# The beginning of a streaming encoder step: meta rows as 128 short rows, gain row spread by a product, forget-gate columns in four blocks, two weight units interleaved

## The reference

```
xn = x * rsqrt(mean(x*x) + 1e-6) * g_pre_mix            # every row, meta rows too
y  = xn @ w_in        # columns: fox q | k | v | 8 forget logits | swa q | k | v | gates
logf = log_sigmoid(f + b_forget);  c = cumsum(logf)      # bias of the fox attention
... fox attention (8 heads), window attention, output mix, MLP
```

## Time and profile before

| what | us |
|---|---|
| median of 3 runs (1680.64 to 1680.95) | 1680.81 |
| the profiled execution, its own time | 1680.76 |
| its span from first to last instruction | 1679.0 |
| TensorE (PE) busy | 1651.5 |
| DVE busy | 1083.5 |
| ACT busy | 775.8 |
| POOL busy | 310.2 |

### The profile page before, as it was taken

The page is one execution under the profiler, slowest core; times in us unless marked ns, Lnnn a source line. Parts: engine busy times, 40 slices in busy tenths (PEclk is TensorE's granted clock), DMA queues, the critical chain, the costliest instruction groups (busy, mean ns, idle before and its releaser), DMA issues.

```text
span 1679.0 us, 27411 instructions
## 1 busy us (share of the span) xinstructions
PE 1651.5 (98%) x9540; PEld 1489.3 (89%) x9540; DVE 1083.5 (65%) x2322; ACT 775.8 (46%) x1630; POOL 310.2 (18%) x438
## 2 busy tenths in 40 slices
PE   8999999999999999999999999999999999999998
PEld 8999999999999988989988899888888888888886
DVE  7556666553999744454445597888877667774744
ACT  6477777765777533352233333222222334443521
POOL 1311111115333211124532230000000000000242
PEclk9999999999999999999999999999999999999999
DMA  5221212231222554563443422444432763444641
GB/s 187 77 61 41 79 47 59 67 110 36 74 57 67 163 179 160 160 210 123 147 140 111 134 85 94 131 144 144 144 131 105 258 220 111 132 149 125 192 163 75
DMA packets 164314, 205.34 MB, mean 122 GB/s; under 512 B 16152, under 2 KB 113240, under 8 KB 164208
## 3 DMA queue, kind: packets, MB, share of 16 engines
q1 hardware_dynamic: 164208, 203.97, 38.0%
HBM read 144.85 MB, written 57.28 MB: 120 GB/s over the span
## 4 chain that ended last, share of the span: by engine, by line
PE 80%; DVE 9%; ACT 4%; issue 4%; POOL 2%; DMA 0%; DVEq 0%; ACTq 0%; SPq 0%; POOLq 0%
PE gb L503 8%; PE gb L3173 6%; PE gb L2290 5%; PE sc L3173 5%; PE gb L2825 4%; PE gb L2661 4%; PE sc L2825 4%; PE tp L3173 4%; PE tp L2825 4%; PE tp L798 3%; PE sc L2449 3%; PE tp L2449 3%; PE gb L930 3%; PE gb L931 2%; PE gb L932 2%
## 5 line engine op out<-in xcount | busy, mean ns | idle before, releaser
L930 PE MATMUL gb<-Xh,wh 128*128 128x384 f32 (+1 forms) x504 | 175.9, 349 | 0.0
L489 POOL TENSOR_TENSOR wl<-raw,wh 128x256 fp32r<-128x256 f32 x168 | 125.0, 775 | 264.2 <-ACT wh L474 175.4
L931 PE MATMUL gb<-Xh,wl 128*128 128x384 f32 (+1 forms) x504 | 170.7, 339 | 0.0
L932 PE MATMUL gb<-Xl,wh 128*128 128x384 f32 (+1 forms) x504 | 170.7, 339 | 0.0
L3297 POOL TENSOR_TENSOR wl<-raw,wh 128x1024 fp32r<-128x1024 f32 x2 | 5.3, 2626 | 559.0 <-ACT wh L3288 559.0
L503 PE MATMUL gb<-Xh,wh 128*128 128x384 f32 (+1 forms) x288 | 103.9, 361 | 0.0
L503 PE MATMUL gb<-Xh,wl 128*128 128x384 f32 (+1 forms) x288 | 97.4, 338 | 0.0
L503 PE MATMUL gb<-Xl,wh 128*128 128x384 f32 (+1 forms) x288 | 97.3, 338 | 0.0
L930 PEld LDWEIGHTS gb<-Xh,wh 128*128 128x128 f32 x504 | 95.0, 189 | 0.1
L931 PEld LDWEIGHTS gb<-Xh,wl 128*128 128x128 f32 x504 | 95.0, 188 | 0.0
L932 PEld LDWEIGHTS gb<-Xl,wh 128*128 128x128 f32 x504 | 94.8, 188 | 0.0
(11 more groups left out here) (548 smaller groups left out, 4777.4 us busy)
## 6 DMA issues: line engine op xcount, KB each, us to landing
zr<-u_scr SPq DMA_DIRECT2D x91, 256.0 KB, 3.0
raw<-in_w_in SPq DMA_DIRECT2D x70, 256.0 KB, 3.2
u_scr<-ustore SPq DMA_DIRECT2D x26, 576.0 KB, 3.6
u_scr<-ustore SPq DMA_DIRECT2D x13, 768.0 KB, 3.2
sig_scr<-sig SPq DMA_DIRECT2D x16, 576.0 KB, 3.1
raw<-in_w_up SPq DMA_DIRECT2D x36, 256.0 KB, 4.4
kc<-in_cache_fox_k SPq DMA_DIRECT2D x8, 1024.0 KB, 5.6
vc<-in_cache_fox_v SPq DMA_DIRECT2D x8, 1024.0 KB, 7.6
```

Of the source, the lines that this page charges most:

```text
L489: nc.gpsimd.tensor_tensor(wl[U.slot][:, q], raw[U.slot][:, q], wh[U.slot][:, q].bitcast(F32), ALU.subtract).then_inc(w_lo if x == 3 else w ...
L930: nc.tensor.matmul(gb[c][:, 0:x1 - x0], wh[U.slot][:, ws], Xh3[:, k, x0:x1], start=(k == 0), stop=False)
L931: nc.tensor.matmul(gb[c][:, 0:x1 - x0], wl[U.slot][:, ws], Xh3[:, k, x0:x1], start=False, stop=False)
L932: last = nc.tensor.matmul(gb[c][:, 0:x1 - x0], wh[U.slot][:, ws], Xl3[:, k, x0:x1], start=False, stop=(k == KT - 1))
```

## The change

Only the beginning of the program changes; from unit 3 on TensorE's instructions are the same, in the same order.

1. The meta tile is laid out as 128 rows of 128 numbers (row = 16 k + r), loaded by ACT's own queue. Its sums of squares are joined over the 8 blocks by a product with a 0/1 matrix (`meta_squares`); it is turned by one transpose in place of eight.
2. The gain row is no longer read 128 times from DRAM (512 KB). One row of 4 KB is loaded, two products with a column of ones spread it over the partitions (`gain_rows`), and DVE copies it out of two banks into `gpre`. For the meta tile 64 KB of it is loaded apart.
3. SP's queue: the first prompt tile ahead of the identity; of the forget columns only 32 in place of 128; unit 1 and unit 2 weights earlier.
4. Chunk 0 of unit 1 is made in two parts: 272 columns once tiles 0 to 2 are there, the other 128 after `gates(0)`.
5. Forget logits: the operands are used as plain fp32, not fp32r; four of the eight blocks lie side by side in the array, each 32 columns wide and each writing its own 32 partitions of the bank (L814). ACT copies all 128 partitions out (`f_sum_act`), and a further fp32 product per chunk adds the four blocks (`f_pick_pe`). No remainder of the weights is made.
6. Units 1 and 2 are interleaved chunk by chunk; `q_keep` and `k_keep` of their chunks move forward into the norm functions.

```diff
@@ norm_sp @@
+            rows_in(1)
             sp.dma_start(ident[:, :], I["cst"][:, C_ID:C_ID + P]).then_inc(id_in, 16)
-            rows_in(0, 1)
-            sp.dma_start(gpre[:, :], I["g_pre_mix"].to_broadcast([P, D])).then_inc(gpre_in, 16)
             rows_in(2, 3)
-            load(sp, Unit(U_F), cols_of(I["w_in"], COL_F))
-            rows_in(4)
-            load(sp, Unit(1), cols_of(I["w_in"], COL_QA))
-            rows_in(5, 6, 7, 8, 9)
+            load(sp, Unit(U_F), f_parts())
+            load(sp, Unit(1), parts_of(1))
+            rows_in(4, 5, 6, 7)
+            load(sp, Unit(2), parts_of(2))
+            rows_in(8, 9)
@@ norm_act @@
+            act.dma_start(xt[0][:, 0:P], I["meta_tokens"].rearrange("r (k f) -> k r f", f=P)).then_inc(x_in[0], 16)
+            act.dma_start(gain_row, I["g_pre_mix"]).then_inc(gpre_in, 16)
...
             square(2)
             square(3)
+            f_copy_act(act)
             root(1)
+            hi(act, Unit(1))
             high(0)
-            f_hi_act(act)
             high(1)
+            high(2)
             square(4)
-            high(2)
-            hi(act, Unit(1))
+            hi_second(act)
             high(3)
             square(5)
             root(2)
+            f_sum_act(act, 0)
             square(6)
             square(7)
             root(3)
             high(4)
+            high(5)
+            q_keep(act, 1, 0, 0)
             square(8)
...
@@ norm_dve @@
+            v.wait_ge(gpre_in, 34)
+            for h in range(2):
+                nc.vector.tensor_copy(gpre[:, 512 * h:512 * h + 512], (gb[0], gb[2])[h][:, :]).then_inc(gpre_in, 1)
             inverse(0)
             newton(0)
-            v.wait_ge(gpre_in, 16)
+            v.wait_ge(gpre_in, 36)
             scaled(0, 1)
             inverse(1)
+            newton(1)
+            scaled(2)
             low(0)
-            newton(1)
-            scaled(2, 3)
             low(1)
             low(2)
+            scaled(3)
             low(3)
...
             scaled(6)
             low(4)
             low(5)
+            lf_dve_z(v, 0)
             scaled(7)
@@ norm_pe @@
+                for k0 in (0, 4):
                     for j, x_ in enumerate((Xh3, Xl3)):
-                        last = nc.tensor.matmul(fbank[c][:, 0:b - a], fw3[:, k, :], x_[:, k, a:b],
+                        for g in range(4):
+                            last = nc.tensor.matmul(fbank[c][32 * g:32 * g + 32, 0:b - a], fw3[:, k0 + g, :],
+                                                    x_[:, k0 + g, a:b].bitcast(F32),
...
+            in_motion(4)
+            gain_rows()
+            meta_squares()
+            in_motion(24)
             turn(0)
             turn(1)
-            in_motion(20)
+            in_motion(16)
             turn(2)
-            turn(3)
-            in_motion(20)
+            in_motion(8)
...
+            tiles_split(3)
+            unit(1, 0, [lambda: None, lambda: turn(3)], (0, THREE))
+            tiles_split(4)
+            gates(0)
+            unit(1, 0, (), (THREE, CHUNK_ALL[0][1]))
+            turn(4)
+            f_pick_pe(0)
+            turn(5)
+            unit(2, 0, [lambda: None, lambda: turn(6)])
+            tiles_split(7)
+            gates(1)
+            unit(1, 1, [lambda: turn(7), lambda: None, lambda: turn(8)])
+            f_pick_pe(1)
+            turn(9)
+            unit(2, 1, [lambda: None, gates_2])
+            f_pick_pe(2)
+            unit(1, 2)
+            unit(2, 2)
```

More of the change, by code:

```diff
@@ L252, in layer @@
         nC = sb("nC", [P, NT], ctx=A2)
+        junk = nC[:, 144:144 + D]
         oT = osT_rl[:, 0:SEQ]
@@ L727, in turn, with gates @@
                     last.then_inc(tp_full, 1)
-            def gates(c, between=()):
+            def gates(c):
                 a, b = CHUNK_ALL[c]
@@ L735, in gates, with f_pick_pe, unit @@
                     pe.wait_ge(bank_free[0], 1)
-                for k in range(KT):
+                for k0 in (0, 4):
                     for j, x_ in enumerate((Xh3, Xl3)):
-                        last = nc.tensor.matmul(fbank[c][:, 0:b - a], fw3[:, k, :], x_[:, k, a:b],
-                                                start=(k == 0 and j == 0), stop=(k == KT - 1 and j == 1))
-                    if k % 2 and k // 2 < len(between):
-                        between[k // 2]()
+                        for g in range(4):
+                            last = nc.tensor.matmul(fbank[c][32 * g:32 * g + 32, 0:b - a], fw3[:, k0 + g, :],
+                                                    x_[:, k0 + g, a:b].bitcast(F32),
+                                                    start=(k0 == 0 and j == 0), stop=(k0 == 4 and j == 1))
                 last.then_inc(gemm_done, 1)
-            def first(c, between=()):
+            def f_pick_pe(c):
                 a, b = CHUNK_ALL[c]
+                pe.wait_ge(f_zero, 3)
+                pe.wait_ge(f_summed, c + 1)
+                nc.tensor.matmul(fbank[c][0:8, 0:b - a], f_pick, f_sums[:, a:b], start=True, stop=True).then_inc(f_picked, 1)
+            def unit(n, c, between=(), only=None):
+                x0 = CHUNK_ALL[c][0]
+                a, b = only or CHUNK_ALL[c]
+                whole = b == CHUNK_ALL[c][1]
                 if c == 0:
-                    pe.wait_ge(w_lo, 2)
-                if c == 2:
+                    pe.wait_ge(w_lo, n + 1)
+                if (n, c) == (1, 2):
                     pe.wait_ge(bank_free[1], 1)
+                elif (n, c) == (2, 2):
+                    pe.wait_ge(bank_free[2], 1)
+                elif n == 2:
+                    pe.wait_ge(bank_free[c], 2)
                 for k in range(KT):
@@ L756, in first, with gain_rows, meta_squares @@
                         between[k // 2]()
-                last.then_inc(gemm_done, 1)
+                if whole:
+                    last.then_inc(gemm_done, 1)
+            def gain_rows():
+                pe.wait_ge(gpre_in, 32)
+                pe.wait_ge(f_zero, 4)
+                for h in range(2):
+                    nc.tensor.matmul((gb[0], gb[2])[h][:, :], ones, gain_row[:, 512 * h:512 * h + 512],
+                                     start=True, stop=True).then_inc(gpre_in, 1)
+            def meta_squares():
+                pe.wait_ge(ssq_done, 1)
+                pe.wait_ge(f_zero, 7)
+                nc.tensor.matmul(meta_sum, same_row, ssq2[:, 0:1], start=True, stop=True).then_inc(f_zero, 1)
             def in_motion(n):
@@ L3507, in _ @@
             norm_act(act)
-            hi_second(act)
-            for c in range(2):
-                q_keep(act, 1, c, 0)
-            f_low_act(act, 2)
             lf_act_(act)
@@ L3614, in _ @@
             lf_dve(v)
-            for c in range(2):
-                k_keep(v, 2, c, 0)
             q_split_dve(v, 0)
             q_zero_dve(v, 0, DH)
-            k_keep(v, 2, 2, 0)
             k_split_dve(v, 0)
@@ L3773, in _ @@
             norm_pe(pe)
-            for n in (2, 3):
-                for c in range(3):
-                    gemm(pe, Unit(n), c, CHUNK_ALL[c])
+            for c in range(3):
+                gemm(pe, Unit(3), c, CHUNK_ALL[c])
             pe.wait_ge(cst_r, 2)
```

131 lines of the change are left out of this document (94 added, 37 removed).

## The result

The changed kernel takes **1703.8 us** (median of 4 runs, 1703.02 to 1705.73), the kernel before 1680.72 beside it (4 runs, 1679.77 to 1680.95): ratio 1.0140, 95% interval 1.0123 to 1.0158. It is slower by 23 us, where 7.5 were forecast. The profiled execution has 1703.02, its span 1701.2 against 1679.0.

A forecast was written before the change was run, and what follows sets the result against it. TensorE, busy for 98% of the span, was taken as the bound. An earlier first product (-1.1), more work (+5.1) and waits (+3.8), given as +7.5 at unit 3's start, made 1688.3 us from 1680.76; range 1684.0 to 1691.0.

The forecast's parts named there:

- Step 1: Start of the kernel: the first product of rows at 18.3, 1.1 us earlier than 19.39.
- Step 2: TensorE's work from the first product of rows to unit 3: +5.1 us for chunk parts, gates, sums and tile 3's turn.
- rival E: Gates (L814): fp32 groups cost what old fp32r products cost per column, 0.18 a group; not slower, 1681.6; chance 0.05.
- Step 3: TensorE's waits up to unit 3: 5.0 us against 1.2, so +3.8, mostly 4.0 ahead of `unit(2, 0)`.
- Rival B: The clock falls in the 4 us wait ahead of `unit(2, 0)`, costing 1.6 us, twice if again in step 1; 1690.0; chance 0.17.
- Unit 3's products still cover its way back, with no slack left (0, up to +1): Behind unit 3's start: the forget sums' store goes out near 75, its return hidden by unit 3's products; 0 to +1 us.
- -1.1 + 5.1 + 3.8: Delay of unit 3's start: earlier first product, added TensorE work and added waits; given as +7.5, 67.7 against 60.29.

The follow-up runs named there:

- the run with the row alone: Changed kernel with the gain's transfers early on SyncE's queue and the gain's 128-row tile on another semaphore than the 4 KB row; 7.3 us below the changed kernel.
- the one before it: Changed kernel with the gain's transfers early on SyncE's queue, ahead of tiles 2 and 3, both still on one semaphore; median 4.2 us below the changed kernel.
- the filled wait: Changed kernel with 34 products whose result nobody reads put into TensorE's wait ahead of `unit(2, 0)`; median 5.1 us below the changed kernel.
- three small edits: Changed kernel with the gain's row alone and early, unit 5's weights ahead of the forget store, and `q_keep` with VectorE's forget part early; 1685.5 us.
- the mended beginning: Changed kernel's beginning with the gain's row early on SyncE's queue and on its own semaphore, also used in later runs; with that edit only, 7.3 us lower.

## Why the prediction was right in direction and wrong in size

The profiled time was forecast at 1688.3 and was 1703.0. In order of time:

**Step 1, the first product of rows: this failed**, by 5.1 us (18.3 against 23.37). The identity landed as worked out (4.79; 4.9). The step then let TensorE go on into the gain products at 5.8, as if the gain were there. Their transfer got no row and no bound: the text gave the time of the identity and of tile 1 and none for the three small transfers on ScalarE's queue. L852 started at 9.45, 3.65 us behind that. It then took 3.71 us, to 13.16, where 3.0 were given with the pace doubling within it; it took the same 3.71 (3.82 to 7.53) where no wait stood ahead. That is 0.7. Another 0.6 is DVE's copying of the gain: the forecast had the first copy run beside the second product and both done 0.75 us behind it, but DVE waits for 34 on `gpre_in`, that is for both products, and was done at 14.47, 1.3 behind them:

```profile
13.27 1.29 DVE L746 COPY gpre<-gb 128x512 f32<-128x512 f32 x2 [7.36 <-PE gb L852]
```

From there to the first product the chain took 8.9 for 8.75. That the wait was one for the gain's transfers, and that the neighbour on the semaphore can hold the row, is shown by the run with the row alone against the one before it, which moved the same transfers in the same order and kept the semaphore.

**Step 2, TensorE's work: right in its prices.** The groups took 0.67 (0.68 forecast), the sums 0.84 and 0.81 on the engine's row, the 128-column products 0.11 each. Against the old gates no time is won; by the traces the old ones are 0.65 us cheaper from the first product on. By the Trainium skill, "TensorEngine Tiling (Array Packing)", section Theoretical Speedup, four blocks side by side could be up to four times as fast. Against plain fp32 one after the other the trace agrees: the sum over the blocks, one fp32 product of the full width and 400 columns, takes 0.77 us from start to start (34.16 to 34.93), and a group of four blocks takes 0.67. Against the fp32r products that the group replaces it doesn't: four of those take 4 x 0.18 = 0.72, and the sums come on top. The gain of the packing is spent on the format, as the forecast said, and rival E was rightly set at 0.05.

**Step 3, the waits: right in the waits, short by the clock.** 3.68 for 4.0 ahead of `unit(2, 0)`, 0.20 for 0.4 ahead of `unit(2, 1)`, 0.27 for 0.4 at unit 3. Rival B (0.17) came on top: 39.70 to 46.71 took 7.0 us for 5.4 at full pace. The whole way from the first product to unit 3 took 51.2 for 49.4, 1.8 more: 1.6 are the clock, and in the rest the waits, 0.85 short of their 5.0, and the work, 1.1 over its 44.4, nearly cancel, which was luck. That it was the clock and nothing else is what the filled wait shows (1.00 for 0.76). It was priced rightly at 1.6 and given too little chance: the forecast knew only a gap of 1.14 us that did no harm and put one of 4 us nearly on its side. The Trainium skill's warning of idle gaps between bursts ("TensorE: Matmul & The Clock Gate", section Why this matters for your kernels) agrees with this trace: 0.76 behind 3.68 us, 0.50 behind 3.44 us. One gap of 3.29 us, in the run with the row alone, left the column at 1.00.

**"Unit 3's products still cover its way back, with no slack left (0, up to +1)": this failed**, by 6.1 us for a forecast of 0 to 1. The step followed the forget sums to the load back and stopped there. It didn't name what was queued behind the store on SyncE, unit 5's weights, nor what stood behind these on ScalarE, the exponentials. The way back was covered, as it said; what was late was the next transfer in the same queue. The store itself was 7.3 us later than forecast (82.29 for 75), of which 6.8 come from the two points above. Of the 6.1 us, 3.4 are the idle time and 2.7 the slower pace behind it, so that the clock took 4.3 of the changed kernel's 23 us in two places. With the one load moved ahead the whole 6.1 us vanished, though the store came even later (84.59).

The rest, 1.3 us, is the late part, which varies by as much in the kernel before. 5.1 + 1.8 + 6.1 + 1.3 = 14.3 of the 14.7 us. A small slip of the sum itself went the same way: its terms, -1.1 + 5.1 + 3.8, make 7.8 and not 7.5. The 0.3 is no rounding; the new start of unit 3 was summed from terms (67.7) and set against the measured 60.29, where the same terms give 59.9.

So the sign was right with two thirds of the loss unforeseen (15.5 of 23 us). Behind the two larger steps lies one omission: transfers were costed where the change removed them (the 512 KB of the gain), and not where it delayed or added them.

## What to carry to other kernels

When work is delayed, follow not only its own result but the next entries of every queue that it passes, the DMA queue's above all: what is issued behind a late store is late too, and so is all that stands behind its first reader. Let a consumer wait for the transfer that it needs and for no other on the same semaphore; the row needed here was there some 4 us before its neighbour (2.6 against 7.0 on SyncE's queue). And where an idle time of several us is forecast on TensorE, put the slower pace behind it into the sum from the start, or fill or reorder it: three small edits here gave back 18 of 23 us, while of the change's own ideas interleaving and parts were worth nothing that shows and the blocks side by side, the short meta rows and the spread gain cost 1 to 3 us.

## What the runs showed of the hardware

- Small transfers can take several us at the start of a kernel, beside large ones: the gain's, issued on ScalarE's queue by 2.9 us, were there at 6.7 (the 4 KB row) and 9.4 (the 128-row tile). The tile, put on SyncE's queue at 2.78 to 3.4, ahead of tiles 2 and 3 and the weights, was there at 7.0, while the row, issued at 1.21, was there at 2.6. The identity, issued at 0.76 with nothing ahead, was there at 2.7. What slows them was not tried apart.
- The granted clock reads 1.00 over the first 20 us in every run, while the identity products of that stretch went at 0.22 a piece at first and 0.11 later: 24 of them took 4.42, 4.98 and 5.36 us in three runs of the same beginning, and with that the first product of rows moved between 23.37 and 24.56; on the mended beginning, 4.20 to 5.36 us and 17.75 to 18.91. In the middle of the kernel the same column shows the lower level plainly (0.50). So at the very start the pace is to be read from the rows, not from the column.
- TensorE's pace can fall with the start behind an idle time or about a us into it: in the changed kernel the products from 39.70 on stood 0.18 apart up to 40.7, then 0.33 apart, and from 44.3 on 0.18 again; in three other runs the first product behind the same wait already took 0.67 for 0.42.
- The same idle time doesn't always cost the same: behind 3.67 to 3.68 us the slower pace cost 1.6 us in two runs and 2.4 to 2.7 in three. Behind 3.44 us (to 96.74) it cost 2.7 and the window shows 0.50; in the same place of other runs it cost 1.7 behind 3.48 us and 2.9 behind 3.30, and 0.2 behind 3.29, with the column at 1.00.
